# The raw input is turned and the token's factor applied behind the first four units; the first half panel comes in two quarters

## What is computed

```python
h = h + even_mixer(rmsnorm(h, ev_norm_mix[i]), ev_w_in[i], ev_conv_a[i], ...)
# rmsnorm(x, g): x * rsqrt(mean(x * x) + eps) * g, a factor for each token, a gain for each feature
# ev_w_in: 1024 x 2048, its output is four parts of 512 columns: h, gb, gc, u
h = h + cross_attn(rmsnorm(h, xa_norm[layer]), mem, xa_norm_mem[layer], xa_wq[layer], xa_wkv[layer], xa_wo[layer])
```

## Time and profile before

| | us |
|---|---|
| median of 3 runs (lowest, highest) | 2174.74 (2174.17, 2175.0) |
| the profiled execution, its own time | 2174.55 |
| its span, first to last instruction | 2172.7 |
| PE busy, share of the span | 2132.4, 98% |
| DVE busy | 1705.5, 78% |
| ACT busy | 1358.0, 63% |
| mean granted TensorE clock | 0.998 |

### The profile page before, as it was taken

The page is one execution under the profiler, slowest core; times in us unless marked ns, Lnnn a source line. Parts: engine busy times, 40 slices in busy tenths (PEclk is TensorE's granted clock), DMA queues, the critical chain, the costliest instruction groups (busy, mean ns, idle before and its releaser), DMA issues. The chain is left out here.

```text
span 2172.7 us, 30889 instructions
## 1 busy us (share of the span) xinstructions
PE 2132.4 (98%) x11990; PEld 1836.0 (85%) x11990; DVE 1705.5 (78%) x1517; ACT 1358.0 (63%) x1163; POOL 96.5 (4%) x109
## 2 busy tenths in 40 slices
PE   8999999999999999999999999999999999999997
PEld 8998999888888888888888888888799888788886
DVE  5755655797588988888888988888866764888887
ACT  5444333536467777777777777777765444577775
POOL 1010000020000000000000000000000000000000
PEclk9999999999999999999999999999999999999999
DMA  9463555574389999999999999999944163699995
GB/s 322 167 179 97 177 198 180 210 213 161 114 300 394 376 394 357 395 373 381 372 382 381 367 387 366 395 357 397 346 167 169 51 225 116 222 378 389 376 377 219
DMA packets 279913, 620.78 MB, mean 286 GB/s; under 512 B 11048, under 2 KB 39920, under 8 KB 279824
## 3 DMA queue, kind: packets, MB, share of 16 engines
q1 hardware_dynamic: 269760, 586.76, 74.0%
q0 software_dynamic: 10064, 32.76, 5.1%
HBM read 603.41 MB, written 12.58 MB: 284 GB/s over the span
## 5 line engine op out<-in xcount | busy, mean ns | idle before, releaser
L2564 DVE TENSOR_TENSOR w_low<-ring,w_high 128x2048 fp32r<-128x2048 f32 x426 | 971.3, 2290 | 130.1 <-ACT w_high L1764 129.0
L1764 ACT ACTIVATE w_high<-ring 128x2048 fp32r<-128x2048 f32 x426 | 815.2, 1917 | 166.9 <-PE ps L851 166.9
L850 PE MATMUL ps<-w_high,parts 128*128 128x512 f32 x1928 | 747.5, 388 | 0.0
L849 PE MATMUL ps<-w_high,parts 128*128 128x512 f32 x1560 | 616.9, 395 | 1.6 <-DVE parts L2244 1.4
L851 PE MATMUL ps<-w_low,parts 128*128 128x512 f32 x1560 | 608.5, 390 | 0.0
L850 PEld LDWEIGHTS ps<-w_high,parts 128*128 128x128 f32 x1928 | 362.5, 188 | 70.3
L1950 DVE TENSOR_TENSOR w_low<-ring,w_high 128x2048 fp32r<-128x2048 f32 (+2 forms) x125 | 280.3, 2255 | 101.7 <-ACT w_high L1485 100.6
L849 PEld LDWEIGHTS ps<-w_high,parts 128*128 128x128 f32 x1560 | 293.1, 188 | 63.9 <-issue 5.9
L851 PEld LDWEIGHTS ps<-w_low,parts 128*128 128x128 f32 x1560 | 292.8, 188 | 62.8
L1485 ACT ACTIVATE w_high<-ring 128x2048 fp32r<-128x2048 f32 (+2 forms) x125 | 235.1, 1885 | 140.1 <-PE ps L851 130.9
L849 PE MATMUL ps<-XT_high,w_high 128*128 128x256 f32 x1088 | 310.9, 286 | 4.7 <-DVE parts L1941 2.9
(11 more groups left out here) (451 smaller groups left out, 1493.1 us busy)
## 6 DMA issues: line engine op xcount, KB each, us to landing
ring<-in_od_moe_gu SPq DMA_DIRECT2D x224, 1024.0 KB, 8.2
ring<-in_od_moe_down SPq DMA_DIRECT2D x112, 1024.0 KB, 8.3
ring<-in_w SPq DMA_DIRECT2D x96, 1024.0 KB, 8.4
ring<-in_ev_ffn_gu SPq DMA_DIRECT2D x22, 1024.0 KB, 6.9
ring<-in_xa_wkv SPq DMA_DIRECT2D x8, 2048.0 KB, 9.2
ring<-in_od_pw_w SPq DMA_DIRECT2D x6, 2048.0 KB, 9.8
ring<-in_w_in SPq DMA_DIRECT2D x6, 2048.0 KB, 8.0
ring<-in_ev_ffn_down SPq DMA_DIRECT2D x11, 1024.0 KB, 5.0
```

The costliest lines, as they stand in the source:

```text
L849: mm(out_, xh, wh, start=start, stop=False)
L850: mm(out_, xl, wh, start=False, stop=False)
L1764: A(w_high[:, j % SPLITS, :], ring[:, j % NS, :], ACT.Copy).then_inc(moe_sem(k, "high"), 1)
L2564: V.tensor_tensor(w_low[:, j % SPLITS, :], ring[:, j % NS, :], w_high[:, j % SPLITS, :].bitcast(F32), SUB)\
```

## The change

x is turned as it is loaded (`turn(H, "x_loaded", 16)`), right behind the first small transpose; the first `keep_busy` is gone and the second has 20 instead of 24. The factor of each token is computed beside that (`factor`, `rsqrt`, `factor_rows("in")`), turned by TensorE behind `in_h` and applied by VectorE to the outputs: its square to h, itself to gb and u. The first half panel is loaded by two DMAs of 128 columns (rows of 512 bytes in place of 1 KB), and each quarter is split by itself; TensorE begins `in_h` with the first. Between the quarters ScalarE and VectorE take the halves of the columns. GpSimd's load of the memory now also waits for `variance_ready`, because the squares use `XS` as scratch. In `memory_projections("A")` the wait for the eviction of `in_gc` stands in front of the turn. Several semaphores are merged (`router_split` and `fox_log`, `fox_sums` and `recurrence_out`, `keys_columns` into `recurrent_keys`), and `xs_ready` counts one less everywhere.

```diff
+        FACTOR = {"in": (w_(8192, T), w_(8448, 2, P)), "ffn": ...}
@@ SyncE
-            sync.dma_start(slot_kn(slot(0))[:, :, 0:T], k_major(ins["ev_w_in"], 0, 0, T)).then_inc(S("first_half_landed"), 16)
+            for quarter, landed_sem in enumerate(("first_quarter_landed", "second_quarter_landed")):
+                n = slice(quarter * P, (quarter + 1) * P)
+                sync.dma_start(slot_kn(slot(0))[:, :, n], ins["ev_w_in"][0, :, n].rearrange("(k p) n -> p k n", p=P)).then_inc(S(landed_sem), 16)
@@ GpSimd
+            pool.wait_ge(S("variance_ready"), 1)
             memory(1, "mem")
@@ TensorE
-                    pe.wait_ge(S("parts_split"), q + 1)
+                    if q == 0:
+                        pe.wait_ge(S("quarter_split"), 1)
+                    else:
+                        pe.wait_ge(S("parts_split"), q + 1)
...
+                            if q == 0 and fb == 1:
+                                pe.wait_ge(S("parts_split"), 1)
...
+                if tag == "A":
+                    evicted("in_gc")
                 turn(XS, ready, value)
                 if tag == "A":
-                    evicted("in_gc")
                     keep_busy(20, 2 * (UNIT["Ak0"] % 2))
...
-            keep_busy(14, 1)
-            turn(XS, "xs_ready", 1)
-            keep_busy(24, 1)
+            turn(H, "x_loaded", 16)
+            keep_busy(20, 1)
             project("in_h", first=True)
...
+            turn_factor("in")
@@ ScalarE
-            rms(H, "x_loaded", 16)
+            squares(H, "x_loaded", 16, XS, True)
...
-            highs(halves_to("in_h", -1))
             act.wait_ge(S("cols_ready"), 1)
-            columns_high(("ev_norm_mix", 0))
+            columns_high(("ev_norm_mix", 0), 0)
+            act.wait_ge(S("first_quarter_landed"), 16)
+            quarter_high(0).then_inc(S("quarter_high"), 1)
+            root()
+            columns_high(("ev_norm_mix", 0), 1)
+            act.wait_ge(S("second_quarter_landed"), 16)
+            quarter_high(1).then_inc(S("parts_high"), 1)
@@ VectorE
-            rms(H, XS, EPS)
-            lows(halves_to("in_h", -1))
+            factor()
             dve.wait_ge(S("cols_ready"), 1)
-            columns_low(("ev_norm_mix", 0))
+            columns_low(("ev_norm_mix", 0), 0)
+            dve.wait_ge(S("quarter_high"), 1)
+            quarter_low(0).then_inc(S("quarter_split"), 1)
+            columns_low(("ev_norm_mix", 0), 1)
+            dve.wait_ge(S("parts_high"), 1)
+            quarter_low(1).then_inc(S("parts_split"), 1)
+            rsqrt()
+            factor_rows("in")
             lows(halves_to("in_gc"))
...
+            factor_row("in")
+            step(V.tensor_tensor(w_(8704, T), FACTOR["in"][0], FACTOR["in"][0], MUL))
+            dve.wait_ge(S("unit_read0"), 1)
+            step(V.tensor_tensor(w_(0, 4, T), w_(0, 4, T), squared, MUL))
+            dve.wait_ge(S("unit_read1"), 1)
+            V.tensor_tensor(w_(1024, 4, T), w_(1024, 4, T), by_token, MUL)
...
-            take_columns("in_u", UP[:, :, 8:264])
+            step(V.tensor_tensor(UP[:, :, 8:264], PAIRS[u % 2].rearrange("p a (b t) -> p (a b) t", t=T), by_token, MUL))
```

More of the change, by code:

```diff
@@ L336, in program @@
         FH, FL = (parts[:, 2 * D + i * 512:2 * D + (i + 1) * 512].rearrange("p (k t) -> p k t", t=T) for i in range(2))
-        FACTOR = {"ffn": (w_(1024, T), w_(1280, 2, P)), "gate": (w_(4352, T), w_(4608, 2, P))}
+        FACTOR = {"in": (w_(8192, T), w_(8448, 2, P)), "ffn": (w_(1024, T), w_(1280, 2, P)), "gate": (w_(4352, T), w_(4608, 2, P))}
         PAIRS = [ps[:, 0:2, :], ps[:, 2:4, :]]
@@ L627, in expert_rows @@
                     pool.dma_start(row_store[k].rearrange("(a p) d -> p a d", p=P), source[:, :, :]).then_inc(S("rows_stored"), 16)
-                    pool.wait_ge(S("xs_ready"), 7)
+                    pool.wait_ge(S("xs_ready"), 6)
                     fill_sums(k, dst)
@@ L672, in _ @@
             row(0, ins["ln_in_g_2"].partition_broadcast(P))
-            expert_rows(1, XS, "xs_ready", 4, H)
+            expert_rows(1, XS, "xs_ready", 3, H)
             loads[1] += 1
@@ L757, in turn_factor @@
             def turn_factor(name):
-                n = 1 + (name == "gate")
-                pe.wait_ge(S("factor_rows"), n)
+                pe.wait_ge(S("factor_rows"), 1 + list(FACTOR).index(name))
                 for tc in range(2):
@@ L947, in _ @@
             last.then_inc(S("small_turned"), 1)
+            turn_factor("in")
             for n in ("gb", "gc", "u"):
                 project("in_" + n)
-            memory_projections("A", "xs_ready", 2)
+            memory_projections("A", "xs_ready", 1)
             pe.wait_ge(S("gain_or_tables_loaded"), 48)
@@ L1035, in _ @@
             project("value1")
-            memory_projections("B", "xs_ready", 3)
+            memory_projections("B", "xs_ready", 2)
             for n in range(KC - DVE_BLOCKS):
@@ L1071, in route @@
                     turn_by_tokens(src, ready, value)
-                pe.wait_ge(S("router_split"), 1)
+                pe.wait_ge(S("small_operands_ready"), 1)
                 E, G = MOES[k]["experts"], MOES[k]["groups"]
@@ L1224, in fox_sums @@
             def fox_sums():
-                pe.wait_ge(S("fox_log"), 1)
+                pe.wait_ge(S("small_operands_ready"), 2)
                 mm(ps[:, 7, 496:500], upto, logf_fox[:, 0, :], start=True, stop=True)
                 mm(ps[:, 7, 500:504], ones, logf_fox[:, 0, :], start=True, stop=False)
-                mm(ps[:, 7, 500:504], upto, logf_fox[:, 1, :], start=False, stop=True).then_inc(S("fox_sums"), 1)
+                mm(ps[:, 7, 500:504], upto, logf_fox[:, 1, :], start=False, stop=True).then_inc(S("small_summed"), 1)
             def fox_scores():
@@ L1291, in diagonals @@
             def diagonals():
-                pe.wait_ge(S("keys_columns"), 1)
+                pe.wait_ge(S("recurrent_keys"), 2)
                 evicted("hq")
@@ L1375, in _ @@
                 last = mm(ps[:, 5, h * P:(h + 1) * P], CR[:, h, :], v(0), start=False, stop=True)
-            last.then_inc(S("recurrence_out"), 1)
+            last.then_inc(S("small_summed"), 1)
             def out_half(j, half, tcs=(0, 1)):
@@ L1393, in out_half @@
                     last.then_inc(S("parts_read"), 1)
-            pe.wait_ge(S("xs_ready"), 5)
+            pe.wait_ge(S("xs_ready"), 4)
             turn_half(0, XS, 2)
@@ L1398, in _ @@
             out_half(1, 0, (0,))
-            pe.wait_ge(S("xs_ready"), 6)
+            pe.wait_ge(S("xs_ready"), 5)
             turn_half(1, XS, 2)
@@ L1478, in highs @@
                     q = n_["high"]
[L1479 to L1482, removed]
+                    wait_panel(act, pieces_split[q][0])
                     if q >= SPLITS:
@@ L1593, in _, with quarter_high @@
             A(table_root, table_root, ACT.Sqrt)
-            rms(H, "x_loaded", 16)
+            squares(H, "x_loaded", 16, XS, True)
             act.wait_ge(S("small_turned"), 1)
             A(cols[:, 0:KC], ps[:, 0, 0:KC], ACT.Copy).then_inc(S("cols_ready"), 1)
-            highs(halves_to("in_h", -1))
             act.wait_ge(S("cols_ready"), 1)
-            columns_high(("ev_norm_mix", 0))
+            def quarter_high(quarter):
+                n = slice(quarter * P, (quarter + 1) * P)
+                return A(half_tile(0, w_high)[:, :, n], half_source(0)[:, :, n], ACT.Copy)
+            columns_high(("ev_norm_mix", 0), 0)
[5 more added lines that the diff above has]
+            quarter_high(1).then_inc(S("parts_high"), 1)
+            n_["high"] = 1
             highs(halves_to("in_gb"))
@@ L1827, in _ @@
             act.wait_ge(S("keys_turned"), 1)
-            A(KH, ps[:, 4:6, :].rearrange("p a (b t) -> p (a b) t", t=T), ACT.Copy).then_inc(S("keys_columns"), 1)
-            act.wait_ge(S("keys_columns"), 1)
+            A(KH, ps[:, 4:6, :].rearrange("p a (b t) -> p (a b) t", t=T), ACT.Copy).then_inc(S("recurrent_keys"), 1)
+            act.wait_ge(S("recurrent_keys"), 2)
             highs(halves_to("hi", -1))
@@ L1904, in factor_row @@
             def factor_row(name):
-                dve.wait_ge(S("factor_turned"), 1 + (name == "gate"))
+                dve.wait_ge(S("factor_turned"), 1 + list(FACTOR).index(name))
                 step(V.tensor_copy(FACTOR[name][0], ps[:, 7, 0:T]))
@@ L2140, in _, with quarter_low @@
             dve.wait_ge(S("x_loaded"), 16)
-            rms(H, XS, EPS)
-            lows(halves_to("in_h", -1))
+            factor()
             dve.wait_ge(S("cols_ready"), 1)
-            columns_low(("ev_norm_mix", 0))
+            def quarter_low(quarter):
+                n = slice(quarter * P, (quarter + 1) * P)
+                return V.tensor_tensor(half_tile(0, w_low)[:, :, n], half_source(0)[:, :, n], half_tile(0, w_high)[:, :, n].bitcast(F32), SUB)
+            columns_low(("ev_norm_mix", 0), 0)
[4 more added lines that the diff above has]
+            quarter_low(1).then_inc(S("parts_split"), 1)
```

(26 more changed lines are left out.)

2 lines of the change are left out of this document (1 added, 1 removed).

## The result

The changed kernel takes 2180.22 us (median of 14 executions, 2179.15 to 2181.26) against 2175.69 (2174.17 to 2176.87) for the kernel before in the same measurement: ratio 1.0021, 95% interval 1.0014 to 1.0028, so 4.5 us (0.2%) slower. The forecast was 2175.4 with a range to 2178.7. The kernel before itself came out 0.95 us above the median of its first three runs, so on the same base the forecast was +0.7 us and the result is +4.5. The profiled execution took 2181.26 us (span 2179.4), the longest of the 14.

The account below looks back on a forecast made before the run. TensorE, busy 98% of the span, was taken as the bound. Start of `in_h` -2.3, `turn_factor` +0.4, idle time +2.5, memory turn +0.1 gave +0.7 us: median 2175.4 from 2174.74, range 2173.5 to 2178.7 (8 in 10).

Parts of the forecast that it names:

- The bound: Before `in_gb`: with panel 1 landing as before, TensorE goes on at 25.84 us, a gain of 0.86 us at most.
- The start: Turn, columns and quarters up to `in_h`: its first product at 12.7 us, 2.3 us earlier than before.
- The two products of `turn_factor`: On TensorE behind `in_h`: some 0.4 us more, up to 24.8 us.
- the landing of panel 1: Weights of `in_gb`: landing at 23.0 us, 1.4 later than before, so `in_gb` starts at 27.3 (bounds 25.9 and 28.1).
- The end of the shared stretch: GpSimd's queue q0 shares the engines with the weights from 14.5 to 21.4 us; panel 1 loses 0.37 MB early on.
- The rows: Smaller 512-byte packets of the first half panel: 0.6 us at most, taken as 0.2 us or 0.08 MB.
- The lag from there to the landing: From panel 1's bytes being complete at 22.4 us to its landing at 23.0: 0.6 us.
- all of q0's load ahead: Upper bound for panel 1's delay: 0.64 MB or 1.6 us, plus 0.6 us for the packets.
- The rival that came true: Idle time before `in_gb` lets TensorE's clock fall: 1.6 us lost, or up to twice that, 2177.0 to 2178.6; chance 0.25.
- Rival 2: Panel 1 isn't late, `in_gb` starts at 25.9 to 26.1 us: 2174.2, at the luckiest 2172.5; chance 0.15.
- Rival 3: 512-byte packets cost as much as 1 KB ones, first half 3.0 us more: 2178.2, with clock over 2180; chance 0.07.
- Behind that: After `in_gb`: third panel at most 0.5 us later, VectorE's 3.2 us covered by 5 us, memory turn +0.1, semaphores 0.

Follow-up runs that it names:

- e12: Kernel before with GpSimd's loads held until ScalarE has panel 1: 2175.92 us against 2176.18 for the kernel before.
- e2: Changed kernel with GpSimd's loads (memory, window table, poolw) held until ScalarE has panel 1: 2173.72 us against 2175.63 for the kernel before.
- e3: Changed kernel with its first half panel in one load of 1 KB rows and GpSimd's loads held behind panel 1: 2173.59 us against 2175.63 before.
- e9: Changed kernel with one load of 1 KB rows and GpSimd's loads held until VectorE has the first quarter: 2174.52 us against 2176.18 before.
- e6: Changed kernel with GpSimd's loads held until half 0 is split: 2173.45 us against 2175.76 for the kernel before.
- e7: Changed kernel with only the window table and poolw held behind panel 1, the memory's load issued early: 2174.76 us against 2175.76 before.
- e1: Changed kernel with its first half panel again loaded by one DMA in 1 KB rows: 2180.55 us against 2175.63 for the kernel before.
- e4: Changed kernel with 40 filler identity transposes behind `turn_factor`, in TensorE's wait for panel 1: 2178.43 us against 2175.63 for the kernel before.
- e5: Changed kernel with GpSimd's loads held until VectorE has the first quarter, 512-byte rows kept: 2178.38 us against 2175.76 for the kernel before.
- e11: Kernel before with its first half panel loaded by two DMAs of 512-byte rows: 2177.32 us against 2176.18 for the kernel before.
- e10: Kernel before with only extra filler transposes at three TensorE waits around 1710 to 1725 us: 2175.82 us against 2176.18 before.

## Why the prediction was wrong

**The bound was read rightly.** With the panel landing as before the gain was capped by the 0.86 us of slack, and everything depended on when that panel lands; e12 shows the slack, and e2 that TensorE follows `in_h` at once when the panel is there.

**The start** was right in its order and off by 1.0 us. `in_h` came at 13.72, not 12.7: the 16 transposes took their 3.67 us (3.5 predicted), but 20 fillers took 3.44 instead of 2.3 us, so the upper clock came 2.4 us later in this execution (12.8 us) than in the trace of before (10.4). Over the runs of the changed start it rose at 10.0 (e3) to 12.9 us (e9), and `in_h` began at 12.26 (e3) to 13.72 us (changed). The two products of `turn_factor` took 0.61 us (0.4 predicted).

**The step that failed is the landing of panel 1**: 23.0 us predicted, with 21.64 to 23.8 as bounds, and 25.49 measured. It has three parts.

- *The end of the shared stretch.* I had q0's bytes from 14.5 to 21.4 us. They came from 15.6 to 22.9, because the issue was at 11.33, not 10.9, and 4.3 us, not 3.6, lie between issue and first bytes (4.1 in the kernel before, where they start at 16.5 and not at 16). Until 22.9 the weights had a third of the rate.
- *The rows.* By 14 us q1 was 0.26 MB behind the kernel before, not 0.08: my line through two larger sizes gave up to 0.6 us, 0.23 MB, and I took a third of that, on the argument that q0's small packets were in the time too, and the argument did not hold. The earlier start of q0 cost another 0.21 MB, not 0.37. The sum of both, 0.47 MB at 20.7 us, is what I had (0.45), by luck. Yet these bytes had to be caught up until 22.9 at the low rate, and so q1 had moved the 5.57 MB up to the end of panel 1 (x 1.05, constants 0.33, two panels of 2.10) at 23.4 us, where I had 22.4; in the kernel before that was at 20.7.
- *The lag from there to the landing.* I took 0.6 us. It was 0.9 in the kernel before, since its bytes were over at 20.7 and not at 21.0, and 2.1 in the changed kernel. It is 0.7 to 1.2 us in e2, e3, e6, e7 and e9, and 2.0 to 2.3 in the changed kernel, e1, e4 and e5, the four with a late share. This is the larger part, 1.5 of the 2.5 us by which the forecast of the landing was short. That the instruction packet makes the share late fits all fourteen traces and was not tested.

My upper bound, "all of q0's load ahead", described what happened: q0's load was over at 22.9. Fourteen of panel 1's 16 shares were there at 24.05 us, near the bound of 23.8; the last two, at 24.71 and 25.47, broke it.

**The rival that came true** is the first: the pause of 3.74 us let the clock fall, at 0.25 of the chances. Its price of 1.6 us was right (1.52 in the trace; by e4's medians 1.8). Its condition was my own forecast's size: with a pause of 2.5 us I had kept it beside the forecast. e5 shows that I should not have: there the pause is 2.24 us and the clock falls all the same (a row of the timeline, and a window):

```profile
28.11 0.39 PE L857 MATMUL ps<-XT_high,w_high 128*128 128x256 f32 x1 [2.24 <-DVE w_low L1968]
...
30.00:32.00 2.00, 2.00 (x11) 2.00 (x11) 0.25 (x1) 1.10 (x1) 0.00 (x0) 0.50 1.05 388
```

The products there run at full rate for 1.3 us, and the clock falls then, at 29.45. Waits of 1.3 us had left the clock alone in the trace of before, 2.2 us did not, and pause and clock belonged into one case. Even waits of 1.3 us are not safe: the falls at 1713 to 1719 us in seven traces come behind one of 1.3 us in a stretch with none longer. With the pause at its predicted 2.5 us that case alone gives 2177; with `in_gb` at the measured 29.78, 2.5 us later than forecast, 2179.5. In e5 the late share decided: by the fifteenth, at 22.78 us, and the same 4.3 us to the first product, the pause would have been 1.2 us (an estimate).

**Rival 2** (panel on time) did not occur at that issue time. Its bound for any luck, 2.2 us under the kernel before, is where the runs with late loads ended: e2, e3 and e6 are 1.9, 2.0 and 2.3 us under it. **Rival 3** (rows) was dismissed by a fair argument and is a smaller matter than I feared for the weights alone (0.7 us, against 3.0 in the rival and 0.2 in the sum), but e5 and e9 put it at 2.6 us in the shared stretch, 0.9 of them for the late share. The one load more costs nothing that the medians tell: e1 is 0.3 us above the changed kernel, e3 0.1 below e2. **Behind that**: the third panel came at 30.88 us (30.75 expected at the latest), and the memory was scaled at 59.6 and turned at 65.94, so its cover of 5 us had become 6; the memory's turn cost 0.23 us, not 0.1; what shows of it is VectorE's wait of 0.32 us behind the step of `in_u`. `evicted("in_gc")` and the merged semaphores cost nothing.

## What to carry to other kernels

When an edit makes an engine faster at the start, list which DMAs it releases, and on which queue; here loads issued 1.5 us earlier on one queue made a panel on another land 3.7 us later (e9, e1), and one wait ahead of those loads (e2, e6) gave back six and a half microseconds. Price a transfer that ends in a stretch shared by two queues by what it still misses, at its part of the rate, and for as long as the sharing lasts. A mean rate gives the middle and not the landing: the load is there when its last share is, and that one can be more than a microsecond late. And when a forecast contains a pause of TensorE longer than any in the trace, the fall of the clock is a part of the forecast, not a rival to it; fillers in the pause (e4) take its cost away and not the pause's.

## What the runs showed of the hardware

- The landing of a 2 MB load moved by 3.7 us when another queue's 1.83 MB were issued 1.46 us earlier (e9, e1): 2.5 us for fifteen of its 16 shares, the rest for the last.
- One packet of instructions, 1.1 us long, starts at 21 to 23 us. The load that is on its way then has its last share 0.8 to 1.5 us behind the fifteenth: panel 1 in the changed kernel, e1, e4 and e5, panel 2 in the other ten traces.
- From GpSimd's issue of a 1 MB load to its first bytes it took 4.1 us (before) and 4.3 (changed).
- Rows of 512 bytes: in the first quarter's stretch, from 8 to 10 us, q1 moved 0.56 MB in e11 against 0.67 with rows of 1 KB in e10, so some 0.28 MB/us against 0.34. For the first half panel of 1 MB this made the landing of panel 1 0.7 us later where the queue was alone (e2, e3).
- TensorE's clock fell after a pause of 2.24 us (e5), 1.3 us after the products had started again, and stayed at its lower level for 3.4 us; it did not fall in e7, with 0.21 us. It rose first at 10.0 to 12.9 us in the runs of the changed start, which moved `in_h` by up to 1.5 us.
